# Start addresses and distances of the stationary sets in a two-block transformer stack (float32r matmuls by high and low parts)

## What is computed

```python
h = rmsnorm(x, g1[l]);  x = x + 0.5 * (silu(h @ w1) * (h @ w3)) @ w2     # D_FF = 2816
h = rmsnorm(x, g2[l]);  x = x + mixer(h) @ w_o
h = rmsnorm(x, g3[l]);  x = x + 0.5 * (silu(h @ w1b) * (h @ w3b)) @ w2b
```

## Time and profile before

| | |
|---|---|
| median of 3 runs | 2453.72 us |
| profiled execution, span from the first to the last instruction | 2447.7 us |
| TensorE busy (modelled) / weight loads busy | 98% / 79% |
| VectorE, ScalarE busy | 55%, 48% |
| DMA, share of 16 engines' span | 51.4% for the weights' queue |
| mean granted TensorE clock | 0.993 |

### The profile page before, as it was taken

One profiled execution on the slowest core, in us unless ns is written; L12 is line 12 of the kernel. 1 busy time (PEld: TensorE's weight loads), 2 busy tenths in 40 slices (PEclk: granted clock), 3 DMA queues, 4 the chain that ended last, 5 costly groups with the idle time before them and its releaser, 6 DMA issues.

```text
span 2447.7 us, 31240 instructions
## 1 busy us (share of the span) xinstructions
PE 2386.8 (98%) x10966; PEld 1939.1 (79%) x10966; DVE 1339.1 (55%) x1470; ACT 1177.9 (48%) x1270; POOL 0.2 (0%) x4
## 2 busy tenths in 40 slices
PE   7999999999999999998999999999999999999999
PEld 5887887887887787886788878788878887878887
DVE  4544565555555456544554566755455446576554
ACT  5444444544544444443544464454454446545543
POOL 0000000000000000000000000000000000000000
PEclk9999999999999999999999999999999999999999
DMA  6556355555556455555455542455555554335553
GB/s 191 175 194 217 130 196 175 186 178 174 183 181 217 143 174 180 180 191 172 155 183 193 168 155 87 159 168 172 197 166 183 185 192 157 102 124 169 189 175 134
DMA packets 311170, 419.14 MB, mean 171 GB/s; under 512 B 16990, under 2 KB 202086, under 8 KB 311048
## 3 DMA queue, kind: packets, MB, share of 16 engines
q1 hardware_dynamic: 306900, 409.26, 51.4%
q10 hardware_dynamic: 4148, 8.34, 1.0%
HBM read 416.50 MB, written 1.05 MB: 171 GB/s over the span
## 4 chain that ended last, share of the span: by engine, by line
PE 85%; issue 4%; DVE 4%; ACT 3%; DMA 3%; SPq 0%; ACTq 0%; DVEq 0%
PE psum L504 26%; PE psum L506 25%; PE psum L505 25%; PE psum L521 3%; DMA raw<-w_in_dram 1%; ACT whi L987 1%; PE psum L753 1%; DVE wlo L1401 1%; PE psum L766 1%; DVE hid L1486 1%; ACT gate L1034 1%; PE psum L594 1%; DMA raw<-w_conv_out_dram 0%; DMA raw<-w_b_dram 0%; PE psum L744 0%
## 5 line engine op out<-in xcount | busy, mean ns | idle before, releaser
L1401 DVE TENSOR_TENSOR wlo<-raw,whi 128x2048 fp32r<-128x2048 f32 (+2 forms) x410 | 895.9, 2188 | 561.8 <-ACT whi L987 554.6
L987 ACT ACTIVATE whi<-raw 128x2048 fp32r<-128x2048 f32 (+2 forms) x411 | 752.0, 1832 | 449.8 <-DMA raw<-w_in_dram 98.7
L504 PE MATMUL psum<-whi,xt_hi 128*128 128x512 f32 (+1 forms) x2176 | 865.3, 398 | 14.1 <-DVE wlo L1401 6.3
L506 PE MATMUL psum<-whi,xt_lo 128*128 128x512 f32 (+1 forms) x2176 | 846.0, 389 | 0.0
L505 PE MATMUL psum<-wlo,xt_hi 128*128 128x512 f32 (+1 forms) x2176 | 844.7, 388 | 0.0
L504 PEld LDWEIGHTS psum<-whi,xt_hi 128*128 128x128 f32 x2176 | 413.5, 190 | 100.3 <-issue 15.5
L506 PEld LDWEIGHTS psum<-whi,xt_lo 128*128 128x128 f32 x2176 | 413.0, 190 | 85.4
L505 PEld LDWEIGHTS psum<-wlo,xt_hi 128*128 128x128 f32 x2176 | 413.9, 190 | 81.7 <-issue 2.9
L504 PE MATMUL psum<-whi,ht_hi 128*128 128x512 f32 x704 | 279.4, 397 | 0.0
L505 PE MATMUL psum<-wlo,ht_hi 128*128 128x512 f32 x704 | 278.1, 395 | 0.0
L506 PE MATMUL psum<-whi,ht_lo 128*128 128x512 f32 x704 | 278.0, 395 | 0.0
(11 more groups left out here) (224 smaller groups left out, 1477.1 us busy)
## 6 DMA issues: line engine op xcount, KB each, us to landing
raw<-w_in_dram SPq DMA_DIRECT2D x180, 512.0 KB, 4.4
raw<-w_a_dram SPq DMA_DIRECT2D x128, 512.0 KB, 4.7
raw<-w_b_dram SPq DMA_DIRECT2D x128, 512.0 KB, 4.7
raw<-ffn_w_gate_dram SPq DMA_DIRECT2D x88, 512.0 KB, 4.0
raw<-ffn_w_up_dram SPq DMA_DIRECT2D x88, 512.0 KB, 5.0
raw<-ffn_w_down_dram SPq DMA_DIRECT2D x80, 512.0 KB, 4.6
raw<-w_o_dram SPq DMA_DIRECT2D x16, 512.0 KB, 4.5
raw<-w_proj_b_dram SPq DMA_DIRECT2D x16, 512.0 KB, 4.3
```

The source lines that it names most:

```text
L504: nc.tensor.matmul(pair(p, m)[:, out], hi[:, c, t], whi[:, slot, w], start=first, stop=False)
L506: last = nc.tensor.matmul(pair(p, m)[:, out], lo[:, c, t], whi[:, slot, w], start=False, stop=final)
L987: nc.scalar.activation(whi[:, u % HL, 0:n], raw[:, u % RAW, 0:n], ACT.Copy).then_inc(hi_done, 1)
L1401: nc.vector.tensor_tensor(wlo[:, u % HL, 0:n], raw[:, u % RAW, 0:n], whi[:, u % HL, 0:n], ALU.subtract).then_inc(w_ready, 1)
```

## The change

Only places and distances in memory change, nothing else. On every engine the instructions and their order are the same, with line numbers one higher.

```diff
-        whi = sb(ctx, "whi", [P, HL, 2048], F32R)
+        whi = sb(ctx, "whi", [P, HL, 2048 + 16], F32R)[:, :, 0:2048]
...
-        xt_hi = sb(ctx, "xt_hi", [P, DC, T], F32R)
-        xt_lo = sb(ctx, "xt_lo", [P, DC, T], F32R)
+        xt_hi = sb(ctx, "xt_hi", [P, DC, T + 4], F32R)[:, :, 0:T]
+        xt_lo = sb(ctx, "xt_lo", [P, DC, T + 4], F32R)[:, :, 0:T]
...
+        sb(ctx, "spacer", [P, 8])
...
-        ht_hi = sb(ffn, "ht_hi", [P, FC, T], F32R)
-        ht_lo = sb(ffn, "ht_lo", [P, FC, T], F32R)
+        ht_hi = sb(ffn, "ht_hi", [P, FC, T + 16], F32R)[:, :, 0:T]
+        ht_lo = sb(ffn, "ht_lo", [P, FC, T + 16], F32R)[:, :, 0:T]
...
-        nc = bacc.Bacc("TRN2", target_bir_lowering=False, num_devices=1)
+        nc = bacc.Bacc("TRN2", target_bir_lowering=False, num_devices=1, dynamic_dma_scratch_size=1024)
```

## The result

The changed kernel takes 2472.11 us (four runs, 2469.93 to 2474.38) against 2454.57 us of the kernel before (four runs too, one more than when the forecast was made). The ratio is 1.0079 with a 95% interval of 1.0065 to 1.0094, so the change makes the kernel 17 to 19 us slower. The forecast was 2434.8 us and the range ended at 2468. The profiled execution took 2473.05 us with a span of 2471.1, so 23.4 us more than the span before.

A forecast was written before the change was run, and what follows sets the result against it. TensorE's step from matmul to matmul was taken as the bound. Terms of -19.2 and +0.3 us, the rest 0, gave -18.9; from the 2453.7 us median that made 2434.8 us, with a range of 2385 to 2468.

The forecast's parts named there:

- What bounds the kernel: Whole kernel: TensorE, busy 98% of the span, so its step from one matmul to the next counts.
- Term 1: ht and mixer matmuls: spacer and ht's 1088-byte distance align 2880 sets to 64 bytes, 19.2 us less.
- Term 2: 96 matmuls of 256 columns (fq and pl): alignment costs 3.3 ns each, 0.3 us more.
- Term 3: Matmuls with x: the 1040-byte distance moves six of eight chunks off multiples of 64; taken as 0.
- upper bound of +31.7: Matmuls with x: 4752 in six chunks paying ht's price of 6.67 ns each, 31.7 us more.
- its sign of being wrong: Matmuls with x: the prediction is wrong if their step moves by more than 2 ns either way.
- Term 4: Weights: whi's slots at 8256 instead of 8192 bytes still start at multiples of 64; 0.
- Term 5: Scratch of 1024 instead of 16384 bytes: hardware queues for weights and tables don't use it; 0.
- Term 6: Weight transfers and ScalarE's copy: they keep up with a faster TensorE, so nothing is given back.
- Rival 1: Matmuls with x: six of eight chunks pay for lost 64-byte alignment, +12.8 us, 2466.5 us; chance 0.20 in full or enough.
- Rival 2: TensorE steps become shorter, down to 2344.6 us; chance 0.25 in some degree, spread between 2344.6 and 2434.
- Rival 3: TensorE steps: something other than 64-byte alignment sets them, no change, 2453.7 us; chance 0.12 with mixtures that cancel.

The follow-up runs named there:

- e2_align: Kernel before with only the 1024-byte scratch and the spacer, no pads: 2438.32 us, ratio 0.9947.
- e8_ht: e2_align plus ht's chunk distance of 1088 bytes: 2442.24 us, ratio 0.9971 to the kernel before.
- e10_after_no_x: The changed kernel with x's pad undone: ratio 1.0076 to the kernel before.
- e9_after_no_whi: The changed kernel with whi's pad undone: ratio 1.0078 to the kernel before.
- e5_weights32: Kernel before with the 1024-byte scratch and 32 bytes in front of whi, moving weights and x's sets together: 2448.72 us, ratio 0.9995.
- e11_pad256: Kernel before with scratch, spacer and pads of 256 bytes for whi, x and ht: 2438.20 us, ratio 0.9962.
- e4_xt: Kernel before with the 1024-byte scratch and x's chunk distance of 1040 bytes only: 2472.87 us, ratio 1.0088.
- e3_whi: Kernel before with the 1024-byte scratch and whi's slots at 8256 bytes only: 2477.04 us, ratio 1.0105.
- e6_slots: Kernel before with the 1024-byte scratch and slots of 8256 bytes for both whi and wlo: 2467.06 us, ratio 1.0073.
- e1_scratch: Kernel before with only the scratch cut to 1024 bytes: 2449.37 us, ratio 0.9994.
- e12_rel16: e2_align with x's and ht's sets 16 bytes further on: 2456.41 us, ratio 1.0034 to the kernel before.
- e7_slots16: e6_slots with x's and ht's sets starting 16 bytes later: 2477.72 us, timed once, against a median of 2449.71.

## Why the prediction was wrong

**What bounds the kernel** was right: nearly all the change is in TensorE's steps, and a shift of 4.1 ns in 6336 of them is 26 us. Clock and copy do not part the steps of the earlier trace rows, as it said: the granted clock is 1.00 in both stretches (111 to 113 and 169 to 171.5 us), TensorE has no idle time there (2.00 of 2.00 and 2.50 of 2.50 us busy), and of the steps with ht from 153.7 to 182.4 us 38 beside ScalarE's copy take 233.2 ns on average and 75 without it 233.3.

**Term 1** (19.2 us less) failed as a term of this change. Its reason was "the same code at such addresses", and "such" meant multiples of 64. The two cases compared differed in the start modulo 64 and in the place relative to the weights alike, and the prediction chose the first. The spacer alone does bring ht to 226.9 ns (e2_align), but ht's own pad (e8_ht: 231.4) undoes it for ht, and whi's and wlo's different places undo it for the mixers (mt at 231.7 in e10_after_no_x, 227.3 in e9_after_no_whi). Measured in the changed kernel: 4.8 us less instead of 19.2.

**Term 2** (0.3 us more for fq and pl) was of the right size with the spacer alone, 116.5 to 119.4 ns in e2_align; in the changed kernel it is some 118, so 0.1 to 0.2 us more.

**Term 3** (0 for x) is the step that failed most: +4.1 ns on all 6336 matmuls, 26.0 us, inside the upper bound of +31.7. The prediction had named this as its sign of being wrong, a move of more than 2 ns. Setting the term to 0, as lying between two bounds, was the error: the only row behind it was x's own step at the old distance, and no run shows a lower bound, a step with x that settles under 226.7 ns. The argument weighed "parts chunks that all lay at the same place" as what can ease a collision. The runs show the opposite: x has its short step, 226.7 ns, where every set lies at place 0 against every stream (before, e5_weights32, e11_pad256), and x's pad takes seven of the eight chunks of xt_hi, and all of xt_lo, off place 0 (e4_xt: 232.2). The prediction also overlooked that xt_lo moves 128 bytes against xt_hi modulo 256.

**Term 4** (0 for whi) failed likewise: this pad alone costs 1.05%. The reason given was that steps don't depend on the slot, but with slots 8192 bytes apart all four have one and the same place modulo 256, so the trace could not show such a dependence. The pad also moved wlo by 256 bytes against whi's first slot; that by itself is harmless (226.7 in slot 0 of e3_whi and of e6_slots). What costs is that slots 1 to 3 of whi come to lie 64, 128 and 192 bytes off wlo's and off the sets' place.

**Term 5** (scratch, 0) was right. **Term 6** (nothing given back) is open in part: e2_align has 17.4 us less in steps and some 13 less in time, e11_pad256 some 9. A share of it goes with the granted clock. Five of six executions of e2_align had 0.990 to 0.992; the one with 0.993 took 2435.85 us, 16.3 less than the mean of the ten executions of the kernel before with 0.993. For e11_pad256 the same comparison (three and five executions) gives 13.1. In the profiled execution of e2_align ScalarE waits 118.4 us for transfers of w_in, where it waited 98.7 before; but it waits 113.3 in the slower changed kernel and 98.9 in e8_ht, so this wait does not follow the step, and why the clock was lower no run shows.

One row beside the terms needs a correction: the 16 matmuls of the pooling product in the earlier trace rows are records, 3.45 us for 16, so 216 ns each. The kernel issues 8 matmuls there, so each float32 matmul of 256 columns leaves two records and takes 431 ns. The 216 ns are no step of a matmul, and no run shows a settled step of 512 float32r columns near them.

**Rival 1** gave 2466.5 us, near the 2472.1, with a mechanism that is refuted by e5_weights32 and by e6_slots, where sets at multiples of 64 have steps from 226.7 to 233.3; chunks 0 and 4 in e4_xt agree with that. Its figure came within 6 us by luck: 231.7 on all chunks costs about as much as 226.7 on two chunks and 233.3 on six, while its -18.9 us for the other tensors was mostly missing. **Rival 2** was wrong in the sign: where pads move sets and weights against each other the step is longer, 231.9 ns with x in e3_whi and 232.2 in e4_xt against 227.6 before. The shorter step behind its 2344.6 us and behind the low end of the range, 2385, no run shows: no settled step was under 226.6 ns, and the fastest kernel took 2438.20 us (e11_pad256). **Rival 3** is out by e1_scratch and e2_align.

What the memory does inside remains unknown: that load and stream wait for one another is inferred from the dependence on their relative place, and no run shows the wait itself.

## What to carry to other kernels

Where float32r matmuls run back to back, each with a new stationary set, read the distance from start to start to the nanosecond: 226.7, 233.3 and an uneven one of 231.7 on average were met with one and the same code here, 2 to 3% of each step, and no busy share shows them. For such matmuls of 512 columns, keep the starts of stationary sets and of the moving pieces equal modulo 256 bytes, for every chunk, slot and part; pads of 256 bytes left the step as it was here (226.7 ns settled, e11_pad256), those of 16 and 64 bytes did not (232.2 ns with x in e4_xt, 231.9 with x in e3_whi, 231.4 with ht in e8_ht). When two rows differ in two ways, a prediction from them needs a run or a row that parts the two: here a shift of both operands by 32 bytes did.

The version that beats both kernels is e2_align, the scratch and the spacer without any pad, at 0.9947 of the kernel before.

## What was not expected of the hardware

- The step settles into repetitions (227 227 226; 236 231 235 231; 232 226 229) that, at most places, are set by the relative place of two operands modulo 256 bytes, and it takes some six to eight steps to get there (318, 231, 236, 228, 233, 231 before 226, 227, 227 in the kernel before, from 106.26 us on). Where the places of high and low weights differ, the sequence is longer but repeats as well (e3_whi).
- One place, 16 bytes, has two settled states, 226.7 and 233.3 ns, in one and the same stage (e12_rel16); 144 bytes seems to be another (e7_slots16).
- Two pads that cost 0.9% (x) and 1.05% (whi) alone cost 0.8% together with ht's pad and the spacer: these harms do not add up.
- With 256 columns the order is reversed: 116.5 ns with sets 32 bytes off (before), 119.4 with sets at place 0 (e2_align).
